# Two attentions of an encoder kernel: probabilities scaled before the turn, values held stationary, scores kept with the sign turned

## What is computed

```
# neighbourhood attention, per head
s = einsum(q, k_window) * scale + bias
p = softmax(s); o = einsum(p, v_window)
# dilated attention, per head; the three groups share one softmax through their denominators
s = einsum(q, k_sel) * scale - slope[g] * abs(offs);  s = where(valid, s, -1e30)
m = max(s); p = exp(s - m); den = sum(p)
out_g = einsum(p / den, v_sel); lse_g = m + log(den)
o = sum(softmax(lse) * out)
```

## Time and profile before

| | |
|---|---|
| time, median of 3 runs | 884.22 us |
| lowest and highest run | 875.2 and 884.54 us |
| the profiled execution: its time | 870.41 us |
| its span, first to last instruction | 868.7 us |
| TensorE busy | 797.4 us (92%) |
| VectorE busy | 599.5 us (69%) |
| ScalarE busy | 422.8 us (49%) |
| GpSimd busy | 71.7 us (8%) |
| mean granted TensorE clock | 0.919 |

### The profile page before, as it was taken

The page is one execution under the profiler, slowest core; times in us unless marked ns, Lnnn a source line. Parts: engine busy times, 40 slices in busy tenths (PEclk is TensorE's granted clock), DMA queues, the critical chain, the costliest instruction groups (busy, mean ns, idle before and its releaser), DMA issues.

```text
span 868.7 us, 17243 instructions
## 1 busy us (share of the span) xinstructions
PE 797.4 (92%) x6580; PEld 750.3 (86%) x6580; DVE 599.5 (69%) x870; ACT 422.8 (49%) x664; POOL 71.7 (8%) x89
## 2 busy tenths in 40 slices
PE   3399998986898999999989999999998999999996
PEld 2299996675788999999979899977787999999995
DVE  3876687779759999874466766667735777776444
ACT  4244464331246666663345444634344666666332
POOL 0200117000200000000020100050000000000000
PEclk9699998577899999999999999995579999999998
DMA  9999885322364999755563898852505576765511
GB/s 360 332 261 330 295 287 194 98 73 81 116 175 122 289 289 290 221 198 207 185 224 134 296 308 296 279 170 76 144 3 146 144 194 193 193 194 194 193 49 48
DMA packets 160047, 171.17 MB, mean 197 GB/s; under 512 B 5178, under 2 KB 142339, under 8 KB 158979
## 3 DMA queue, kind: packets, MB, share of 16 engines
q1 hardware_dynamic: 151363, 139.11, 51.0%
q0 software_dynamic: 8640, 31.46, 10.2%
HBM read 169.50 MB, written 1.05 MB: 196 GB/s over the span
## 4 chain that ended last, share of the span: by engine, by line
PE 79%; DVE 12%; DMA 5%; issue 2%; ACT 1%; SPq 1%; POOLq 0%; DVEq 0%; ACTq 0%
PE acc L1049 50%; PE big L1049 14%; DMA ada_raw<-in_ada_w 4%; PE aux L1178 2%; DVE mod_acc L774 2%; DVE mod_acc L714 2%; DVE qk L287 2%; PE big L1318 2%; PE aux L1101 1%; PE big L1201 1%; PE acc L1206 1%; PE acc L1330 1%; DVE w_lo L704 1%; PE big L1323 1%; PE acc L1112 1%
## 5 line engine op out<-in xcount | busy, mean ns | idle before, releaser
L1049 PE MATMUL acc<-h_hi,w_hi 128*128 128x256 f32 x1248 | 351.4, 282 | 17.3 <-DVE h_lo L754 14.8
L1049 PE MATMUL acc<-h_lo,w_hi 128*128 128x256 f32 x1248 | 348.6, 279 | 0.0
L1049 PE MATMUL acc<-h_hi,w_lo 128*128 128x256 f32 x1248 | 348.6, 279 | 0.0
L704 DVE TENSOR_TENSOR w_lo<-w_raw,w_hi 128x1024 fp32r<-128x1024 f32 x220 | 263.1, 1221 | 105.0 <-ACT w_hi L474 104.9
L474 ACT ACTIVATE w_hi<-w_raw 128x1024 fp32r<-128x1024 f32 x220 | 224.5, 1050 | 101.3 <-PE big L1049 62.4
L1049 PEld LDWEIGHTS acc<-h_hi,w_hi 128*128 128x128 f32 x1248 | 238.4, 191 | 19.6 <-issue 17.7
L1049 PEld LDWEIGHTS acc<-h_lo,w_hi 128*128 128x128 f32 x1248 | 238.1, 191 | 0.4
L1049 PEld LDWEIGHTS acc<-h_hi,w_lo 128*128 128x128 f32 x1248 | 237.8, 191 | 0.0
L714 DVE SCALAR_TENSOR_TENSOR mod_acc<-ada_raw,cact,mod_acc 128x1024 f32<-128x1024 f32 x80 | 106.8, 1338 | 21.8 <-DMA ada_raw<-in_ada_w 21.6
L1049 PE MATMUL big<-hid_hi,w_hi 128*128 (+1 forms) x352 | 97.2, 276 | 0.0
L1049 PE MATMUL big<-hid_lo,w_hi 128*128 (+1 forms) x352 | 97.2, 276 | 0.0
(11 more groups left out here) (184 smaller groups left out, 911.8 us busy)
## 6 DMA issues: line engine op xcount, KB each, us to landing
w_raw<-in_ffn_w_up SPq DMA_DIRECT2D x88, 512.0 KB, 5.0
ada_raw<-in_ada_w POOLq DMA_DIRECT2D x60, 512.0 KB, 5.6
w_raw<-in_ffn_w_down SPq DMA_DIRECT2D x44, 512.0 KB, 4.0
w_raw<-in_odd_w_in SPq DMA_DIRECT2D x40, 512.0 KB, 5.0
w_raw<-in_even_w_in SPq DMA_DIRECT2D x32, 512.0 KB, 6.0
ada_raw<-in_ada_w SPq DMA_DIRECT2D x20, 512.0 KB, 3.8
ada_first<-in_ada_w SPq DMA_DIRECT2D x5, 1024.0 KB, 8.1
w_raw<-in_even_w_out SPq DMA_DIRECT2D x8, 512.0 KB, 5.2
```

The source lines that it names most:

```text
L704: dve.tensor_tensor(w_lo[:, n % SPLIT, part], w_raw[:, n % RAW, part], w_hi[:, n % SPLIT, part].bitcast(F32), ALU.subtract).then_inc(s_lo, 1)
L1049: ins = pe.matmul(dst, lhsT, rhs, start=start and n == 0, stop=stop and n == 2, skip_group_check=True)
```

## The change

- The signs: scores are kept negated. The bias step computes minus scale times score minus bias, the row minimum takes the place of the maximum, and exp is given scale -1, so that the minimum serves as its bias and the negation (L841) is gone.
- The slopes: the ratio of the groups' slopes goes into the table of distances, so the dilated bias is one instruction over 384 columns, not three.
- The scaling: VectorE multiplies the probabilities (128x256 or 128x384, in SBUF) by the reciprocal of their sum, two steps behind the scores. The scaling of the result out of `acc` (L833) and the tiles `ntok`, `ctok` are gone.
- The turn of the probabilities waits for that scaling and stands three steps behind the scores, no longer two; the multiplication with values stands four behind.
- The operands: values (128x64) are stationary and the turned probabilities (128 columns) move. The result comes out with features on partitions, odd heads on partitions 64 to 127, in banks 2 and 3 of `big`. The turn L1195 and its waits are gone.
- The scores have two banks, no longer three.
- ScalarE places a pair of heads by one copy of 128x256 in four steps, in place of two of 128x128.

```diff
-C_SLOPE = C_DIST + TT * ROW
-C_INV = C_SLOPE + 2 * C_HEADS
+C_INV = C_DIST + TT * ROW
...
+        flatter = np.array([slope(g, 0) / slope(0, 0) for g in range(C_GROUPS)])[group]
...
-        a[:, C_DIST + t * ROW:C_DIST + (t + 1) * ROW] = np.where(ok, off, BIG)
-    for h in range(C_HEADS):
-        a[:, C_SLOPE + 2 * h] = np.where(half, -slope(2, h), -slope(1, h))
-        a[:, C_SLOPE + 2 * h + 1] = np.where(half, -slope(1, h), -slope(2, h))
+        a[:, C_DIST + t * ROW:C_DIST + (t + 1) * ROW] = np.where(ok, off * flatter, BIG)
...
-            def attend(base, scores, kept, tokens, placed, beside=lambda s: None):
+            def attend(base, scores, kept, placed, beside=lambda s: None):
 
                 width = scores.shape[2]
-                for s in range(STEPS + 7):
+                for s in range(STEPS + 5):
                     if s < STEPS:
                         act.wait_ge(shifted, base + s + 1)
-                        nc.scalar.activation(scores[:, s % 4, :], scores[:, s % 4, :], ACT.Exp,
+                        nc.scalar.activation(scores[:, s % 4, :], scores[:, s % 4, :], ACT.Exp, scale=-1.0,
                                              bias=stat[:, s % 4, 1:2], accum_out=stat[:, s % 4, 2:3]).then_inc(exp_done, 1)
-                    if 0 <= s - 2 < STEPS:
-                        r = s - 2
+                    if 0 <= s - 3 < STEPS:
+                        r = s - 3
                         act.wait_ge(turned, base + r + 1)
                         if r >= 2:
                             act.wait_ge(attended, base + r - 1)
                         nc.scalar.activation(kept[:, r % 2, :], aux[:, r % 2, 0:width], ACT.Copy).then_inc(probs_kept, 1)
-                    if s >= 7 and (s - 6) % 2:
-                        j = (s - 6) // 2
-                        act.wait_ge(out_turned, base // 2 + j + 1)
-                        nc.scalar.activation(placed(j), tokens(big[:, 3, 0:P]), ACT.Copy).then_inc(out_placed, 1)
+                    if s >= 8 and s % 4 == 0:
+                        pair = s // 4 - 2
+                        act.wait_ge(attended, base + 4 * pair + 4)
+                        placed(pair, big[:, 2 + pair % 2, 0:T]).then_inc(out_placed, 1)
                     beside(s)
 
-            attend(0, ns, npt, lambda a: a, lambda j: work[:, 4 + j // 2, (j % 2) * P:(j % 2 + 1) * P])
+            attend(0, ns, npt, lambda pair, got: nc.scalar.activation(work[:, 4 + pair, :], got, ACT.Copy))
...
-            attend(STEPS, cs, cpt, lambda a: a.rearrange("p (r b) -> p r b", r=2),
-                   lambda j: by_residue(work[:, j // 2, :])[:, 2 * (j % 2):2 * (j % 2) + 2, :],
+            attend(STEPS, cs, cpt,
+                   lambda pair, got: nc.scalar.activation(by_residue(work[:, pair, :]),
+                                                          got.rearrange("p (r b) -> p r b", r=RES), ACT.Copy),
...
-            def attend(base, scores, tok, shift, beside=lambda s: None):
-
-                for s in range(STEPS + 4):
-                    if s >= 4:
-                        r = s - 4
-                        j = r // 2
-                        dve.wait_ge(exp_done, base + r + 1)
-                        link(dve.reciprocal(stat[:, r % 4, 3:4], stat[:, r % 4, 2:3]))
-                        dve.wait_ge(attended, base + r + 1)
-                        if r % 2 == 0 and j >= 2:
-                            dve.wait_ge(out_turned, base // 2 + j - 1)
-                        dve.tensor_scalar(tok[:, j % 2, (r % 2) * DH:(r % 2 + 1) * DH], acc[:, r % 2, 0:DH],
-                                          stat[:, r % 4, 3:4], None, ALU.mult).then_inc(out_taken, 1)
+            def attend(base, scores, shift, beside=lambda s: None):
+
+                for s in range(STEPS + 2):
                     if s < STEPS:
                         dve.wait_ge(scored, base + s + 1)
                         if s >= 4:
                             dve.wait_ge(turned, base + s - 3)
                         link(shift(s, 2 * (s // 4) + s % 2, s // 2 % 2))
-                        link(dve.tensor_reduce(stat[:, s % 4, 0:1], scores[:, s % 4, :], AX_X, ALU.max))
-                        dve.tensor_scalar(stat[:, s % 4, 1:2], stat[:, s % 4, 0:1], -1.0, None,
-                                          ALU.mult).then_inc(shifted, 1)
+                        dve.tensor_reduce(stat[:, s % 4, 1:2], scores[:, s % 4, :], AX_X, ALU.min).then_inc(shifted, 1)
+                    if s >= 2:
+                        r = s - 2
+                        dve.wait_ge(exp_done, base + r + 1)
+                        link(dve.reciprocal(stat[:, r % 4, 3:4], stat[:, r % 4, 2:3]))
+                        dve.tensor_scalar(scores[:, r % 4, :], scores[:, r % 4, :], stat[:, r % 4, 3:4], None,
+                                          ALU.mult).then_inc(probs_scaled, 1)
                     beside(s)
 
             def nat_shift(s, h, t):
 
                 e = 2 - 2 * t
-                return dve.scalar_tensor_tensor(out=ns[:, s % 4, :], in0=big[:, s % 3, 0:T], scalar=SCALE,
-                                                op0=ALU.mult, op1=ALU.add,
+                return dve.scalar_tensor_tensor(out=ns[:, s % 4, :], in0=big[:, s % 2, 0:T], scalar=-SCALE,
+                                                op0=ALU.mult, op1=ALU.subtract,
                                                 in1=nbias[:, h, e:e + 4, :].rearrange("p e c -> p (e c)"))
 
             def dil_shift(s, h, t):
 
-                for at0, at1, k in ((0, T, -slope(0, h)),
-                                    (T, T + 64, consts[:, C_SLOPE + 2 * h:C_SLOPE + 2 * h + 1]),
-                                    (T + 64, ROW, consts[:, C_SLOPE + 2 * h + 1:C_SLOPE + 2 * h + 2])):
-                    col = C_DIST + t * ROW
-                    ins = dve.scalar_tensor_tensor(out=cs[:, s % 4, at0:at1], in0=consts[:, col + at0:col + at1],
-                                                   scalar=k, in1=big[:, s % 3, at0:at1], op0=ALU.mult, op1=ALU.add)
-                return ins
+                col = C_DIST + t * ROW
+                return dve.scalar_tensor_tensor(out=cs[:, s % 4, :], in0=consts[:, col:col + ROW], scalar=slope(0, h),
+                                                in1=big[:, s % 2, 0:ROW], op0=ALU.mult, op1=ALU.subtract)
...
-            def attend(base, width, scores_of, values_of, kept, tok, values_at, beside=lambda s: None):
-
-
-                for s in range(STEPS + 6):
+            def attend(base, width, scores_of, values_of, kept, values_at, beside=lambda s: None):
+
+
+                for s in range(STEPS + 4):
                     if s < STEPS:
-                        if s >= 3:
-                            pe.wait_ge(shifted, base + s - 2)
-                        scores_of(big[:, s % 3, :], 2 * (s // 4) + s % 2, s // 2 % 2).then_inc(scored, 1)
+                        if s >= 2:
+                            pe.wait_ge(shifted, base + s - 1)
+                        scores_of(big[:, s % 2, :], 2 * (s // 4) + s % 2, s // 2 % 2).then_inc(scored, 1)
                     beside(s)
-                    if 0 <= s - 2 < STEPS:
-                        r = s - 2
-                        pe.wait_ge(exp_done, base + r + 1)
+                    if 0 <= s - 3 < STEPS:
+                        r = s - 3
+                        pe.wait_ge(probs_scaled, base + r + 1)
                         if r >= 2:
                             pe.wait_ge(probs_kept, base + r - 1)
                         for j in range(width // P):
                             ins = pe.transpose(aux[:, r % 2, j * P:(j + 1) * P],
                                                (ns if base == 0 else cs)[:, r % 4, j * P:(j + 1) * P], ident)
                         ins.then_inc(turned, 1)
-                    if 0 <= s - 3 < STEPS:
-                        r = s - 3
+                    if 0 <= s - 4 < STEPS:
+                        r = s - 4
+                        h, t = 2 * (r // 4) + r % 2, r // 2 % 2
                         if r == 0:
                             pe.wait_ge(z_evicted, values_at)
                         pe.wait_ge(probs_kept, base + r + 1)
-                        if r >= 2:
-                            pe.wait_ge(out_taken, base + r - 1)
-                        values_of(acc[:, r % 2, 0:DH], kept[:, r % 2, :], 2 * (r // 4) + r % 2,
-                                  r // 2 % 2).then_inc(attended, 1)
-                    if s >= 6 and s % 2 == 0:
-                        j = (s - 6) // 2
-                        pe.wait_ge(out_taken, base + 2 * j + 2)
-                        if j >= 1:
-                            pe.wait_ge(out_placed, base // 2 + j)
-                        pe.transpose(big[:, 3, 0:P], tok[:, j % 2, :], ident).then_inc(out_turned, 1)
+                        if r >= 8 and r % 4 == 0:
+                            pe.wait_ge(out_placed, (base + r) // 4 - 1)
+                        lane = slice((h % 2) * DH, (h % 2 + 1) * DH)
```

(29 more changed lines are left out.)

2 lines of the change are left out of this document (1 added, 1 removed).

## The result

| | before | after |
|---|---|---|
| time, median | 879.71 us (4 runs, 869.89 to 884.54) | 900.88 us (4 runs, 899.85 to 902.14) |
| the profiled execution | 870.41 | 902.14 |
| its span | 868.7 | 900.1 |
| mean granted clock | 0.919 | 0.923 |

The ratio is 1.0325, with a 95% interval of 1.0266 to 1.0384: the changed kernel is slower by about 21 us (31.7 us between the two profiled executions). I had forecast 889, with 896 as the upper end.

What follows compares the result with a forecast made beforehand. TensorE at the low clock bounds steady steps, VectorE the heads. Terms +0.4 + 3.6 + 0.7 + 0 - 0.6 + 1.0 = +5.1 us give 875.5 profiled, 889 from the median 884.2; range 866 to 896.

Steps and rivals of the forecast that it cites:

- My sum: All stretches of both attentions added up: +5.1 us on the profiled 870.4; no term for the dense multiplications.
- Steady part of the first attention: Nine TensorE-bound steps at the low clock: 2.72 us each (2.62 to 2.93) instead of 2.62, +0.4 in all.
- Steady part of the second: Eight TensorE-bound steps at the low clock: 3.87 to 3.97 us each instead of 3.98, taken as 0.
- Head of the first attention: VectorE's scaling is held by GpSimd's products, so the seventh scores start at 154.0 instead of 150.36: +3.6 us.
- Tail of the first: After the last scores, turn and values stand one step further behind: 8.4 us against 7.69, +0.7.
- Head of the second: VectorE's savings pay for held scalings; eighth scores at about 590.6: -0.6 us, bounds -2 and +2.
- Tail of the second: From the last scores to the pooling matmuls: 12.0 us against 11.00, +1.0.
- Rival 1: Granted clock rises to 1.00 inside the attentions, VectorE then bounds: 870 us (second only) or 864 (both); chance 0.25.
- Rival 2: TensorE pays nothing for the shape change and the head's scaling is never held: about -2.5, 882 us; chance 0.18.
- Rival 3: With two score banks, late additions delay minimum and scores: 0.4 us on 25 steps, +10, above 899; chance 0.04.
- Rival 4: The shape change between turn and values costs its upper bound: +0.2 on 30 steps, +6 more, 895 us; chance 0.08.

Runs made afterwards that it cites:

- padded kernel: The changed kernel with 16 unused columns (64 bytes a partition) put back into its constants, restoring the old addresses behind them: 882.94 us, ratio 1.0034.
- the shifted kernel before: The kernel before with one small tile moved so that the tiles behind it lie 64 bytes lower, no operation changed: 895.13 us, ratio 1.0223.
- the run with one shape: The padded kernel with the values' stationary operand 128x128 like the turn's, instead of 128x64 (output not the reference's): 879.73 us.
- after_same: The changed kernel run again without any change, beside the kernel before: 898.3 us, ratio 1.025.
- the other paddings: The changed kernel with other numbers of unused columns in its constants; 32 columns took 904.36 us, 48 took 894.19 us.
- no_scale: The padded kernel with only one column of the probabilities scaled, the division by the sum left out (output not the reference's): 862.75 us.
- three_banks2: The padded kernel with a third bank for the scores again, timed in ten runs: 869.67 us, ratio 0.9917 to the kernel before.
- spread: As three_banks2, with the second attention's two long splits on VectorE issued in halves over four steps: 874.87 us.

## Why the prediction was wrong, point by point

**The step that failed** is the inventory of the change. My sum costed instructions and took the lines of the diff that drop the slope columns as a table that gets smaller. They also move every tile behind the constants by 64 bytes. I priced the dense multiplications, 64% of the chain of waits, at nothing without saying so, and no rival touched them. Their term is +20 us in the two networks and about 25 with the projections between them, from one profiled execution to the other. Between the medians of the unpadded and the padded kernel it is 15 us. The padded kernel shows it from one side (ratio 1.0034), the shifted kernel before from the other (1.0223). No row that I had read could have given the price, but the move itself stood in the diff.

**The rest of the sum was near.** It said +5.1 us; the padded kernel's ratio of 1.0034 is +3 us, and its interval goes from -5 to +11. In the changed kernel's own profile the two attentions grew by 3.5 and 3.7, where I had +4.7 and +0.4. That the total came near is in part luck, since in the second attention an error of +5.6 in the head and one of -3.1 in the tail cancel in part:

- *Steady part of the first attention*: 2.81 a step against 2.72 predicted, nine steps +1.3 against +0.4. Values of four at 1.05 with the change of shape, where I had 0.85 + 0.10: the shape costs 0.19. The Trainium skill (TensorEngine Tiling (Array Packing), Key Properties) says that a change of the tiling mode drains TensorE; the run with one shape agrees, by 0.19 us a step and by the load that starts earlier.
- *Steady part of the second*: 4.08 against 3.97, eight steps +0.8 against 0. L1314 stayed at 0.43.
- *Head of the first attention*: right in mechanism, near in size. The seventh scores came at 153.24 (154.0 predicted), 15.3 us after the first where the earlier trace rows has 12.56: +2.7 against +3.6. The scaling was held twice, once longer than drawn (1.99 us) because it met GpSimd's instruction just as that began. The size is partly luck: in the second profile of the changed kernel (after_same) the first of these scalings took 0.46 us, and the seventh scores came 13.8 us after the first, +1.2; with the other paddings it was 12.4 to 15.8. Alone the scaling takes 0.35 and 0.42 us, where I had 0.29 and 0.36. The Trainium skill (SBUF — State Buffer, Who interferes with whom) says that an instruction of VectorE within SBUF may take the port pair shared with GpSimd and that the other is then blocked; 1.99 us against 0.35 agrees.
- *Tail of the first*: 7.2 us against 7.69, so -0.5 where I had +0.7. The work is as I had counted it, but the clock rose at about 185, so the last values ran at half the price, and the recurrence's first matmul L1214 (185.81) already stands among them:
```profile
183.73 1.05 PE big L1187 x4
184.78 0.45 PE aux L1164 x2
185.22 0.80 PE big L1187 x5
```
- *Head of the second*: I had -0.6 by bounds of -2 and +2. The eighth scores came 24.1 us after the first (591.11 to 615.18) against 19.04: +5.0, beyond both bounds. With two banks the third scores waited for a late addition (1.35 us), the clock was at 0.50 from about 594.5 to 601.3 behind that gap, and the modulation sum L1098 next to them took 6.04 us where before it took 3.61. The gap does not always cost the clock: no_scale has one at the same place (third scores 2.9 us after the first) and kept 1.00.
- *Tail of the second*: 8.9 us against 11.00, -2.1 where I had +1.0, since the clock rose at about 652 inside it.

**Rivals.** Rival 1 (another clock level) did not decide the changed kernel: its clock was 0.50 in both steady parts and rose only in the two tails and for 7 us in the second's head. The level it spoke of was reached in other variants, by a clock that did not fall: the second attention took 47.3 us in three_banks2 and 46.0 in no_scale, 14.6 and 15.9 less than before, where I had priced it at 19. Its dilated step at 1.00 is near (2.30 against 2.4), but the bound is not what I wrote: TensorE, not VectorE, fills a step without a split. Rival 2 (nothing paid) is refuted by 2.81 and 1.99 us. Rival 3 (the score loop closes) occurred at the third dilated scores and in no steady part; I had charged it to 25 steps. Rival 4 (shape at its upper bound, 0.31) lies further from the 0.19 measured than my 0.10 does.

## What to carry to other kernels

Read a diff for what it moves in memory as well as for what it runs: a table made shorter by 64 bytes shifted the operands of untouched multiplications and cost 20 us, almost three times the 7.2 that the edited stages added in the profiled execution. When a kernel's longest stage changes pace at equal counts and without waits, compare operand addresses and try a pad before looking for a reason in the edit. And measure small changes against several runs of before, since one of its stages may have two paces of its own.

## What the runs showed of the hardware that I had not expected

- In float32 matmuls of 128x128 by 256 columns, the pace depends on the distance between the stationary and the moving operand's addresses: 0.1133 us each at best with 192 bytes (mod 256), 0.1183 with 224, 0.1187 with 128 (0.1200 in one network), 0.1200 with 0. These are the x528 pieces of the second matrix of each network, and the granted clock was 1.00 in them.
- At a distance of 192 there are two levels, 0.1133 and 0.1178, that can change between two stages of one execution (59.84 and 62.20 us for the same 528); at 64 only 0.1178 was seen.
- The second attention can keep 1.00 to its end though TensorE waits in it (no_scale, three_banks2), while once at 0.50 in its steady steps it stayed there until the last scores or longer: 2.30 against 4.08 us a step.
- The busy time of TensorE just ahead does not tell whether the granted clock falls: it was 0.73 of 2 us ahead of a fall in after_padded, 1.07 in spread and 1.22 in the kernel before, while no_scale kept the clock with 0.95 and three_banks2 with 1.28.
